# Eight raw weight buffers and expert 0 outside of the ranking in a mixture of 32 experts

## What is computed

```python
def _moe_ffn(x2d, router_w, router_b, w_gu, b_gu, w_down, b_down):
    logits = (x2d @ router_w + router_b).astype(jnp.float32)
    top_val, top_idx = lax.top_k(logits, TOP_K)
    gate = jax.nn.softmax(top_val, axis=-1)
    ...
    def expert_block(args):
        xblk, e = args
        hg, hl = jnp.split(xblk @ w_gu[e] + b_gu[e], 2, axis=-1)
        hg = jnp.minimum(hg, SWIGLU_LIMIT)
        hl = jnp.clip(hl, -SWIGLU_LIMIT, SWIGLU_LIMIT)
        glu = hg * jax.nn.sigmoid(hg * SWIGLU_ALPHA)
        return ((hl + 1.0) * glu) @ w_down[e] + b_down[e]
```

## Time and profile before

| | us |
|---|---|
| median of 3 runs | 3335.88 (3333.21 to 3338.71) |
| profiled execution, its time | 3340.06 |
| profiled execution, its span | 3338.4 |
| PE busy | 3142.1 (94%) |
| DVE busy | 2090.2 (63%) |
| ACT busy | 1598.1 (48%) |

### The profile page before, as it was taken

One profiled execution on the slowest core, in us unless ns is written; L12 is line 12 of the kernel. 1 busy time (PEld: TensorE's weight loads), 2 busy tenths in 40 slices (PEclk: granted clock), 3 DMA queues, 4 the chain that ended last, 5 costly groups with the idle time before them and its releaser, 6 DMA issues. The chain is left out here.

```text
span 3338.4 us, 48173 instructions
## 1 busy us (share of the span) xinstructions
PE 3142.1 (94%) x18749; PEld 2360.6 (71%) x18749; DVE 2090.2 (63%) x2549; ACT 1598.1 (48%) x1942; POOL 207.8 (6%) x202
## 2 busy tenths in 40 slices
PE   8999899898999999999999998999999999999998
PEld 6876567484747474747767776788887877778886
DVE  6745758393938383838568866566537876565633
ACT  4424336373737373737457446354326536544422
POOL 0000001121212121212000000000000000000000
PEclk9998989999999999999999999999999999999999
DMA  4103249999999999999322110232322121122231
GB/s 150 62 29 103 91 175 361 405 354 413 360 407 352 410 350 410 354 413 365 125 67 71 64 59 25 82 101 95 107 89 70 66 69 39 53 87 95 95 107 64
DMA packets 117708, 600.37 MB, mean 180 GB/s; under 512 B 19490, under 2 KB 23090, under 8 KB 67138
## 3 DMA queue, kind: packets, MB, share of 16 engines
q1 hardware_dynamic: 105442, 580.57, 46.3%
q0 software_dynamic: 12096, 17.40, 2.1%
HBM read 582.62 MB, written 27.33 MB: 183 GB/s over the span
## 5 line engine op out<-in xcount | busy, mean ns | idle before, releaser
L2807 DVE TENSOR_TENSOR wl<-raw,wh 128x2048 fp32r<-128x2048 f32 x240 | 546.1, 2286 | 75.2 <-ACT wh L2721 74.3
L2721 ACT ACTIVATE wh<-raw 128x2048 fp32r<-128x2048 f32 x240 | 459.5, 1916 | 193.7 <-PE pu L2627 73.6
L4695 ACT ACTIVATE w_high<-w_raw 128x1024 fp32r<-128x1024 f32 (+1 forms) x114 | 131.2, 1151 | 319.4 <-PE acc L4667 161.1
L2625 PE MATMUL pu<-wh,Xh 128*128 128x512 f32 x640 | 260.2, 407 | 16.2 <-DVE wl L2807 16.2
L4742 DVE TENSOR_TENSOR w_low<-w_raw,w_high 128x1024 fp32r<-128x1024 f32 (+1 forms) x114 | 152.4, 1337 | 185.1 <-PE ps L4625 99.8
L4647 PE MATMUL ps<-x_high,w_high 128*128 128x512 f32 x656 | 255.2, 389 | 0.0
L4648 PE MATMUL ps<-x_low,w_high 128*128 128x512 f32 x656 | 255.2, 389 | 0.0
L2627 PE MATMUL pu<-wh,Xl 128*128 128x512 f32 x640 | 254.1, 397 | 0.0
L2626 PE MATMUL pu<-wl,Xh 128*128 128x512 f32 x640 | 253.6, 396 | 0.0
L3499 PE MATMUL acc<-x_high,w_high 128*128 128x512 f32 x528 | 219.5, 416 | 3.0 <-ACT hq L3905 1.5
L3500 PE MATMUL acc<-x_low,w_high 128*128 128x512 f32 x528 | 207.4, 393 | 0.0
(11 more groups left out here) (895 smaller groups left out, 6941.3 us busy)
## 6 DMA issues: line engine op xcount, KB each, us to landing
raw<-in_exp_w SPq DMA_DIRECT2D x312, 1024.0 KB, 8.0
more_raw<-in_exp_w SPq DMA_DIRECT2D x72, 1024.0 KB, 17.8
w_raw<-in_w_in SPq DMA_DIRECT2D x100, 512.0 KB, 3.4
w_raw<-in_w_up SPq DMA_DIRECT2D x82, 512.0 KB, 3.7
w_raw<-in_w_down SPq DMA_DIRECT2D x32, 704.0 KB, 4.0
w_raw<-in_w_out SPq DMA_DIRECT2D x32, 384.0 KB, 3.1
kv_raw<-in_w_mem_kv SPq DMA_DIRECT2D x16, 512.0 KB, 3.7
x<-in_x SPq DMA_DIRECT2D x4, 1024.0 KB, 7.8
```

Of the source, the lines that this page charges most:

```text
L2625: nc.tensor.matmul(o, lh[:, k, :], wh[:, m % PARTS, c], start=(m >= 8 and kh == 0 and kk == 0), stop=False)
L2721: nc.scalar.activation(wh[:, m % PARTS, :], raw[:, m % RAW, :], ACT.Copy).then_inc(w_high, 1)
L2807: nc.vector.tensor_tensor(wl[:, m % PARTS, :], raw[:, m % RAW, :], wh[:, m % PARTS, :], ALU.subtract).then_inc(w_low, 1)
```

## The change

There are eight slots for raw chunks instead of six: `raw` keeps its 6 slots (`HELD`), and two more, `spare_raw`, lie in the first block's tile `y`. All wide units and the ring part of the pairs go round these eight in turn; `off` and `turn` of a unit say where in the ring it starts. A loop turn takes 48 ring chunks, six rounds. In a pair the order becomes 8 ring chunks, 8 `more_raw`, 4 ring, 4 `more_raw`.

Expert 0 is taken out of the ranking. It is always the first unit, gets rank 31, and has its own small mask, positions and gates (`routed0`, `pos_first`, `gfirst`). SP loads its chunks without waiting for `order`; the wait for `order_ready` stands after them. The selection, the index and the constants for the first unit move ahead of the ranking's second half on DVE, `slots` of the first unit ahead of the ranking on PE, and POOL loads its biases right after the gather.

```diff
-RAW = 6
+HELD, RAW = 6, 8
...
-    unit(Unit(0, 0, FEW, one, 0, 0, first=True), Unit(1, 1, FEW + 1, 2 * one, 1, 0))
+    unit(Unit(0, 0, EXPERTS - 1, one, 0, 0, 0, 0, first=True), Unit(1, 1, FEW, 2 * one, 1, 0, 0, 12))
...
+        spare_raw = place_y[:, :, :].rearrange("p (a b) n -> p a (b n)", a=2)
...
+            def slot_of(n, c):
+
+                v = (n.off + c) % RAW
+                where = raw[:, v, :] if v < HELD else spare_raw[:, v - HELD, :]
+                return where, loaded[v], n.turn * 96 + (16 * ((n.off + c) // RAW) + 16)
...
-                            elif c < 2 * RAW + 2 * PARTS:
+                            elif c < RAW + 2 * PARTS + 4:
                                 sp.wait_ge(used, n.at * CHUNKS + ((c - RAW - 2 * PARTS) // 2 + 1))
                             else:
-                                sp.wait_ge(used, n.at * CHUNKS + ((c - 2 * RAW - 2 * PARTS) // 2 + 6))
+                                sp.wait_ge(used, n.at * CHUNKS + (c // 2 - 3))
...
-                    e = expert_at(n.rank)
+                    e = 0 if n.first else expert_at(n.rank)
                     for m in range(CHUNKS):
                         if m < RAW and n.behind:
-                            sp.wait_ge(used, n.at * CHUNKS + (m // 2 + 8 - CHUNKS))
+                            sp.wait_ge(used, n.at * CHUNKS + ((m // 2 + 3 if m < 4 else m // 2 + 7) - CHUNKS))
                         elif m >= RAW or not n.first:
                             sp.wait_ge(w_low, n.wide * CHUNKS + (m - RAW + 1))
-                        chunk_in(e, m, m % RAW)
+                        chunk_in(e, m, slot_of(n, m))
+                    if n.first:
+                        sp.wait_ge(order_ready, 1)
 
                 sp.dma_start(b_down[:, :], b_in).then_inc(down_in, 16)
-                sp.wait_ge(order_ready, 1)
                 all_units(sp, unit)
...
                     if n.first:
                         gather(0, 0)
+                        pool.wait_ge(ones_ready, 5)
+                        bias_of(n)
                         pool.wait_ge(late_taken, 2)
                         pool.dma_start(spill, spill_rows).then_inc(spilled, 16)
-                        pool.wait_ge(ones_ready, 5)
                         pool.wait_ge(order_ready, 1)
-                        bias_of(n)
...
                     elif n.behind:
-                        act.wait_ge(used, n.at * CHUNKS + ((4, 5, 11, 12)[m] - CHUNKS))
+                        act.wait_ge(used, n.at * CHUNKS + ((5, 6, 11, 12)[m] - CHUNKS))
```

More of the change, by code:

```diff
@@ L2308, with __init__ @@
 class Unit:
-    def __init__(self, at, wide, rank, bias, odd, pairs, pair=False, behind=False, first=False, last=False):
-        self.at, self.wide, self.rank, self.bias, self.odd, self.pairs, self.pair = at, wide, rank, bias, odd, pairs, pair
+    def __init__(self, at, wide, rank, bias, odd, pairs, turn, off, pair=False, behind=False, first=False, last=False):
+        self.at, self.wide, self.rank, self.bias, self.odd, self.pairs, self.turn, self.off, self.pair = at, wide, rank, bias, odd, pairs, turn, off, pair
         self.behind, self.first, self.last = behind, first, last
@@ L2330, in all_units, with mixture @@
         unit(a3, a4)
-    unit(Unit(UNITS - 1, WIDE - 1, EXPERTS - 1, one + (3 * one + two) * PAIRS + one, 1, PAIRS, last=True), None)
-def mixture(K, a, x, gates, kept, saved, gain, shift):
+    unit(Unit(UNITS - 1, WIDE - 1, EXPERTS - 2, one + (3 * one + two) * PAIRS + one, 1, PAIRS, PAIRS, 12, last=True), None)
+def mixture(K, a, x, place_y, gates, kept, saved, gain, shift):
     nc = K.nc
@@ L2427, in pair_slot @@
                     again = v % PARTS >= 2
[L2428 to L2432, removed]
-                return more_raw, v, more_loaded[v], n.pairs * 32 + 32
+                    return more_raw[:, v, :], more_loaded[v], (n.pairs * 32 + 16) if again else (n.pairs * 16 + 16)
+                if c < RAW + 2 * PARTS + 4:
+                    return slot_of(n, c - 2 * PARTS)
+                v = w[c - RAW - 2 * PARTS]
+                return more_raw[:, v, :], more_loaded[v], n.pairs * 32 + 32
             def halves(m):
@@ L2489, in _, with bias_rows @@
             def _(pool):
-                def bias_rows(rank, row):
-                    e = pool.value_load(order[0:1, bass.ds(rank, 1)], min_val=0, max_val=EXPERTS - 1)
+                def bias_rows(rank, row, first=False):
+                    e = 0 if first else pool.value_load(order[0:1, bass.ds(rank, 1)], min_val=0, max_val=EXPERTS - 1)
                     for g in range(4):
@@ L2643, in pair_chunk @@
                         begin, end = m >= 8 and kh == 0 and kk == 0, kh == 1 and kk == 3
-                        nc.tensor.matmul(o[0:HALF, :], lh[:, k, 0:HALF], raw_l[:, left, c], start=begin, stop=end)
-                        mm = nc.tensor.matmul(o[HALF:SLOTS, :], lh[:, k, HALF:SLOTS], raw_r[:, right, c], start=begin, stop=end)
+                        nc.tensor.matmul(o[0:HALF, :], lh[:, k, 0:HALF], left[:, c], start=begin, stop=end)
+                        mm = nc.tensor.matmul(o[HALF:SLOTS, :], lh[:, k, HALF:SLOTS], right[:, c], start=begin, stop=end)
                         if kk == 3:
@@ L2667, in _ @@
                 mm.then_inc(gates_turned, 1)
+                slots(first)
                 pe.wait_ge(picked, 1)
@@ L2679, in _ @@
                                  start=False, stop=True).then_inc(placed, 1)
-                slots(Unit(0, 0, FEW, 64, 0, 0, first=True))
                 pe.wait_ge(late_ready, 2)
@@ L2713, in high_part @@
                 def high_part(n, m):
-                    act.wait_ge(loaded[m % RAW], chunk_loaded(n, m))
+                    piece, arrived, count = slot_of(n, m)
+                    act.wait_ge(arrived, count)
                     if m >= PARTS:
```

112 lines of the change are left out of this document (67 added, 45 removed).

## The result

| | before | after |
|---|---|---|
| median of 5 runs, us | 3335.88 | 3314.3 |
| range, us | 3333.21 to 3342.62 | 3309.0 to 3323.14 |
| profiled execution, us (span) | 3340.06 (3338.4) | 3309.0 (3307.4) |
| ratio after / before | | 0.9928, 95% interval 0.9907 to 0.9949 |

The change makes the kernel faster by 21.6 us by the medians. In time the interval of the ratio reaches from 17 to 31 us, and the forecast of 27 us less (3309) lies in it. The two profiled executions are 31.0 us apart, more than the medians, so I read lengths of turns and of units from them, and not the difference of their spans.

What follows compares the result with a forecast made beforehand. The bound alternates each turn: DMA late in the pair, PE in wide units, linked by chunks loadable ahead. Pairs 25.9 us (5.0 + 20.9) plus start 1.0 gave 27 us, median 3335.88 to 3309; forecast gain 20 to 31 us, chance 0.66.

Steps and rivals of the forecast that it cites:

- The lead, first pair: First pair of the mixture: two more chunks landed before PE's first chunk, thanks to expert 0's early loads; 5.0 us gained.
- The lead, five more turns: Later turns: lead refilled in DMA idle time after the stall; 4.2 us each, 20.9 us in all, range 2.9 to 5.0 each.
- The start: First unit: earlier bias rows win at most 1.6 us, less 0.6 us added to the chain; 1.0 us gained, bounds -1 to +4.
- B: Wide units: no DMA headroom, so the lead is filled only once; 6 us gained, 3330 us; chance 0.10.
- C: `behind` units: deeper load queue makes the two-scatter chain 2 us longer each; 15 us gained, 3321 us; chance 0.14.
- D: `behind` units: scatter chain much longer, 6 us lost in each, 36 lost against 27 gained; 3345 us; chance 0.04.
- A: All six pairs: full 5.0 us lead in each turn plus 4 at the start; 34 us gained, 3302 us; chance 0.06.
- A turn of 167.3 us: Mixture loop: the turn from pair to pair takes about 167.3 us instead of 171.5.
- The share after the stall of 0.98 or more: Window after the `behind` unit's stall: DMA share 0.98 or more instead of 0.85 to 0.90; forecast wrong if under 0.92.
- PE's waits in the pair's second part under 1 us: Second part of the pair: PE waits less than 1 us, where it waited 4.7.
- The biases end no wait: Start of the first unit: bias rows no longer end a wait of PE, which was 2.35 us.
- SP's waits for `wl` shrink by 20 us: SP's load queue: its waits for DVE's `wl` to free weight slots shrink by some 20 us.

Runs made afterwards that it cites:

- late loads: After kernel with eight slots, but SP issues expert 0's loads only when the ranking is done; ratio to before 0.9924, 3314.48 us.
- second profiles: The kernels before and after, each unchanged and profiled once more; 3330.93 us and 3306.12 us.
- half loads: After kernel in which each wide-unit load behind the first unit brings half of its chunk's columns, engines' work unchanged; 3274.36 us, one run.
- lead of six: After kernel with all eight slots, but SP's waits let it run only six chunks ahead in wide units; ratio to before 1.0007.
- half loads with the move: After kernel with half of the columns loaded in wide units, and `pay` taken at chunk 11 instead of 8; 3260.22 us, one run.
- six slots: After kernel with six raw slots and the old ring and waits again, expert 0 still first and outside the ranking; ratio to before 0.9994.

## Why the prediction was right, point by point

**The lead, first pair.** Predicted 5.0 us, measured 50.75 to 46.98 in the pair and 4.4 us by the turn's length (171.48 to 167.09). So the term was 0.6 to 1.2 us too large. That two more chunks of lead shorten the pair holds; the reason given for their being there (the early loads of expert 0) does not, as the kernel with late loads shows.

**The lead, five more turns.** Predicted 4.2 us each. The starts of the pairs in the two profiles move apart by 2.5, 5.2, 6.8, 4.6 and 3.5 us in turns two to six (the last one counted up to the last unit), 22.6 us against 20.9. With the second profiles the turn is 171.3 against 167.3 us in the mean, 4.1 us. The term was sized by the DMA's share after the stall, and this was a good measure: shares of 0.85 to 0.90 became 0.97 in the first turn, and the landing time there went from 4.8 to 8.5 us. But it was not what ended the gain. With half loads, where the DMA has time to spare, the pairs are no shorter than in after, 46.2 us in both. What ended it is the lead of eight itself, worth 2.2 to 2.3 us a chunk and not 2.48, close above a limit which the prediction had not named: PE's own 45.1 us in a pair. The DMA's idle time just sufficed. That its 4.2 us lie so near to the 4.6 by which the mean pair fell (50.8 to 46.2) is in part luck.

**The start.** Predicted 1.0 us with bounds of -1 and +4, measured 2.1. The wait for the bias rows did go, and `Xl` did come next. The wrong term is the 0.6 us that the prediction added to the chain and took off the 1.6: the chain became shorter. From the copy of the gates to the end of `Xl` it is 25.72 us before and 24.97 after (25.65 and 25.05 in the second profiles), and PE then starts on the bias rows 0.15 us behind `Xl` instead of 1.56: 0.7 and 1.4 us, together 2.1. The gather goes out 7 us earlier (487.24 instead of 494.30), but PE comes to its rows at 503.18 instead of 503.75, since in after the rows have landed 8.6 us behind the issue, at about 496, and PE has other work in its list until then. This is why so early a gather brought so little.

**The sum.** 27 us predicted. In the profiles, the mixture's last unit starts 29.0 us earlier: 27.0 from six turns and 2.0 from the start. Another 2.0 us lie behind the mixture, where the code is the same. By the medians it is 21.6 us, at the low side, with 27 inside the interval. Before's profiled execution was 4.2 us above its median and after's was the fastest of its five runs; this is where 31 and 21.6 part.

**The rivals.** B (no headroom) falls: the pairs 2 to 6 gain as much as the first. C and D (longer scatters) fall for this change: the second scatter of the first pair is issued 10.36 us behind the first one in both kernels, DVE's wait for POOL is 6.54 us against 6.39, and over the mixture it is 42.7 us against 41.6 (44.3 against 39.4 in the second profiles), where C needed 12 us more. Their mechanism does exist, though. The half loads cut DVE's waits for the scatters from 42.7 to 17.6 us, so the scatters' time does depend on the loads beside them. It depends on how many bytes are moved meanwhile, and those windows were at 1.02 before and after, not on how deep SP's queue is. A (the full lead in each turn) was nearer in its mechanism than I gave it credit for, since the pairs are as short as with half loads. Its size falls: a chunk of lead is worth 2.3 us and the start 2.1 instead of 4, and its 34 us lie outside of the measured 17 to 31.

**The signs.** A turn of 167.3 us: measured 166.8 and 167.7. The share after the stall of 0.98 or more: 0.97, 0.98, 0.98, 1.01 and 0.97 in the 30 us behind the five stalls (before: 0.85 to 0.90), so it held in three of five and was narrowly missed in two. PE's waits in the pair's second part under 1 us: 1.58 in the first pair, 0.63 in the whole of the third. The biases end no wait: right. SP's waits for `wl` shrink by 20 us: wrong. In the five turns from the first pair's start to the sixth's SP's waits for DVE are these in before (583.25 to 1440.83),

```profile
SPq L2445 <- DVE wl L2807: 417.0, 150, 11.2
SPq L2460 <- DVE wl L2807: 72.1, 30, 4.1
```

and this in after (581.24 to 1415.33):

```profile
SPq L2452 <- DVE wl L2820: 486.5, 180, 11.2
```

So 489.1 became 486.5 us. SP waits for the same subtractions of DVE as before, only two chunks further ahead. The shorter turns show in SP's waits for PE in the pairs, 176.5 to 157.5 us.

**What the prediction missed.** It treated the stall of the `behind` unit as a given, and as the hole in which the lead is filled. By the medians the stall was the larger prize, 37 us against 22. Without it most turns are 163 to 165 us with six slots or eight, and the two changes don't add in full: the slots' 4 us a turn need the time which the stall leaves to the DMA. What the slots still bring then lies in the first pair.

## What to carry to other kernels

This rests on one kernel. Where the bound changes hands between phases, price a deeper prefetch as the smaller of three numbers: the lead in loads times the time of one load, the idle time of the DMA in the phase that refills it, and the distance to the compute engine's own busy time in the phase that uses it. Look first, though, for a step in an in-order engine's list that waits for something late while others wait behind it, as `pay` did here: to move it costs no memory, and it gave 37 us (interval 29 to 42) where two more buffers and the new start gave 22 (17 to 31). And compare starts from a landmark at the stage's beginning, since absolute times drift by microseconds from profile to profile.

## What the runs showed of the hardware

A DMA share of 1.00 does not say that nothing is left. Turns with a share of 1.00 moved 391 to 397 GB/s, and turns of the same traffic with 1.01 moved 394 to 403. The rate tells more than the share near the top.

In several profiles PE begins one unit late, with no releaser that the profile shows, and its matmuls run at a lower clock behind it. In the second profile of after, PE at 1377.03 us:

```profile
1377.03 0.80 PE L2604 MATMUL pu<-brow,ones 32*128 32x512 f32 x4 [3.70 <-issue]
```

That unit took 38.30 us where the same unit takes 35.95 in other turns (granted clock 0.75 in its first 12 us), and the turn is 5.7 us longer than the other four. Such waits, 1.15 to 3.70 us long and always at the start of the third wide unit of a turn, stand 12 times in nine of the thirteen profiles (three times in that of the lead of six, twice in that of half loads with the move), but not in the two of before, the first of after and that of the six slots.

This unit is the first one behind the end of the loop's body, where PE branches back (L2320). The rows of that line show what goes with the wait, in the second profile of after (1369.2 us) and then in the first (1373.9 us), durations in ns:

```profile
L2320 PEldq COMPARE_BRANCH  x1: 7557/7557/7557, 1369.2 to 1369.2; - x1
```

```profile
L2320 PEldq COMPARE_BRANCH  x1: 208/208/208, 1373.9 to 1373.9; - x1
```

In all 12 cases this branch of PE took 4.8 to 7.6 us, and up to the next branch the trace has nine transfers of 16 KB on the queue for instructions. In the other 53 turns it took 0.21 to 0.25 us, and there is no such transfer up to the next branch. So PE begins late where the loop's instructions are brought in again. Why this comes in some turns and not in others stays open: the code is the same, and of two profiles of after one has it and the other not. It is of the size of the gains discussed, so the mean of a few turns of one profile is not safe without a look for it.
